# Last norm of the sample rows over 128 lanes of 256 columns, and their accumulating loads moved ahead of two prompt tiles

## What is computed

```
x = layer_norm(ALPHA * x + hier_moe(x, p), p['ln3_g'], p['ln3_b'])

def layer_norm(x, g, b):
    mu = xf.mean(-1, keepdims=True)
    var = jnp.mean(jnp.square(xf - mu), -1, keepdims=True)
    return (xf - mu) * lax.rsqrt(var + LN_EPS) * g + b
```

## Time and profile before

| | |
|---|---|
| median of 3 runs | 645.8 us (643.83 to 647.42) |
| the profiled execution | 641.11 us, span 639.4 us |
| mean granted clock of TensorE | 0.993 |
| busy, share of the span | PE 96%, DVE 57%, ACT 26%, POOL 32% |
| the chain that ended last, by engine | PE 76%, DVE 8%, DMA 7%, POOL 3% |
| DMA | 150.08 MB, mean 235 GB/s |

### The profile page before, as it was taken

How to read it: one execution, slowest core, us unless ns; L and a number is a source line. 1 busy time by engine, 2 the same in 40 slices (tenths; PEclk the granted TensorE clock), 3 DMA queues, 4 the chain that set the end, 5 groups by cost and what they waited for, 6 DMA issues and landing times.

```text
span 639.4 us, 9069 instructions
## 1 busy us (share of the span) xinstructions
PE 612.1 (96%) x3369; PEld 395.5 (62%) x3369; DVE 366.1 (57%) x847; ACT 163.7 (26%) x367; POOL 202.1 (32%) x248
## 2 busy tenths in 40 slices
PE   8999999999999999999999999999999999999992
PEld 5688788887788854446888774444574443333230
DVE  2476797327465863657553965356885342443465
ACT  1094401102553120002002640221433111211144
POOL 7040100101678735412001985011325731110231
PEclk9999999999999999999999999999999999999997
DMA  8995488706436354004705985453998999999898
GB/s 275 361 375 201 167 204 234 258 2 213 120 115 216 114 198 149 16 0 172 289 1 174 332 292 192 163 221 145 375 417 324 406 411 392 342 411 417 331 185 174
DMA packets 49181, 150.08 MB, mean 235 GB/s; under 512 B 5501, under 2 KB 8257, under 8 KB 44903
## 3 DMA queue, kind: packets, MB, share of 16 engines
q1 hardware_dynamic: 35159, 112.48, 47.2%
q0 software_dynamic: 11232, 31.76, 17.3%
q10 hardware_dynamic: 2744, 5.23, 2.2%
HBM read 131.83 MB, written 21.90 MB: 240 GB/s over the span
## 4 chain that ended last, share of the span: by engine, by line
PE 76%; DVE 8%; DMA 7%; POOL 3%; issue 2%; SPq 2%; ACT 1%; DVEq 0%; POOLq 0%; ACTq 0%
PE ps L618 16%; PE ps L797 14%; PE ps L1158 9%; PE ps L616 8%; PE ps L1178 6%; PE ps L517 5%; DMA xn<-in_x_sample 3%; PE ps L816 2%; PE ps L1196 2%; PE ps L899 2%; PE ps L591 2%; PE ps L883 2%; DMA P<-x_d,smp 1%; SPq L1284 1%; PE ps L1139 1%
## 5 line engine op out<-in xcount | busy, mean ns | idle before, releaser
L797 PE MATMUL ps<-wring,P 128*128 128x512 f32 x224 | 99.2, 596 | 0.0
L797 PEld LDWEIGHTS ps<-wring,P 128*128 128x128 f32 x224 | 41.6, 190 | 49.1 <-issue 49.0
L1938 DVE SCALAR_TENSOR_TENSOR P<-ps,P 128x256 f32<-128x256 f32 (+1 forms) x83 | 33.8, 424 | 56.6 <-PE ps L618 36.5
L1158 PE MATMUL ps<-wring,P 128*32 128x512 f32 (+1 forms) x320 | 63.5, 593 | 0.9 <-DVE P L2613 0.9
L517 PE MATMUL ps<-xT,wring 128*128 128x312 f32 (+1 forms) x256 | 57.4, 383 | 0.0
L517 PEld LDWEIGHTS ps<-xT,wring 128*128 128x128 f32 x256 | 46.4, 190 | 9.3
L2613 DVE COPY P<-ps 128x512 f32<-128x512 f32 x10 | 6.9, 692 | 64.7 <-PE ps L1139 64.7
L1158 PEld LDWEIGHTS ps<-wring,P 128*32 128x32 f32 (+1 forms) x320 | 20.4, 122 | 30.9 <-issue 30.9
L2935 POOL TENSOR_TENSOR P<-P,xT 128x2048 f32<-128x2048 f32 x8 | 36.1, 4522 | 8.8 <-DMA xT<-sq_d 5.4
L2787 POOL TENSOR_SCALAR rstd<-agg 128x1 f32<-128x1 f32 (+1 forms) x10 | 11.9, 1195 | 82.8 <-DVE agg L1867 82.8
L2246 DVE SCALAR_TENSOR_TENSOR xn<-xn,ps 128x512 f32<-128x512 f32 x16 | 11.0, 684 | 39.6 <-PE ps L797 29.0
(11 more groups left out here) (484 smaller groups left out, 1152.6 us busy)
## 6 DMA issues: line engine op xcount, KB each, us to landing
wring<-in_w_in SPq DMA_DIRECT2D x5, 2048.0 KB, 9.6
wring<-in_w_gate SPq DMA_DIRECT2D x10, 1024.0 KB, 8.3
wring<-in_w_up SPq DMA_DIRECT2D x10, 1024.0 KB, 11.2
P<-in_w_down SPq DMA_DIRECT2D x10, 1024.0 KB, 12.6
P<-in_cache_mem_k SPq DMA_DIRECT2D x8, 1024.0 KB, 6.8
P<-in_cache_mem_v SPq DMA_DIRECT2D x8, 1024.0 KB, 5.4
y_d<-P POOLq DMA_DIRECT2D x1, 4160.0 KB, 31.7
wring<-in_ca_wv SPq DMA_DIRECT2D x2, 2048.0 KB, 19.7
```

Source lines behind the costliest of these rows:

```text
L797: last = mm(bk[:, :], src[:, k, START[t]:START[t] + TR], w[:, k, :], start=(k == 0), stop=(k == KC - 1))
L1158: last = mm(GU[p % 2][lo:lo + m, :].rearrange("p (g f) -> p g f", g=2), xgT[:, p % 3, k, lo:lo + m], gu[s][:, :, k, :], start=(k == 0), st ...
L1938: V.scalar_tensor_tensor(dst, src, scale, part, ALU.mult, ALU.add).then_inc(part_added, 1)
```

## The change

- The samples' last norm is done on 128 partitions: row r's quarter g of 256 columns lies on partition 32g + r (the tile samples_s). SP moves the four quarters there from xn (four DMAs inside the on-chip memory) once the samples' second choice has landed. POOL clears samples_s earlier, and loads the gain in the same layout by four DMAs.
- VectorE adds the samples' sums straight from PSUM in one instruction of 128x256; mean, square and centring are one instruction of 256 columns each. The sums over the four quarters of a row are made by TensorE with a 0/1 matrix (same_lane, made in place_rows), once for the mean (after the sums of tile 1) and once for the variance (before the sums of tile 4): sum_lanes. The copies L1801 and L2700 are gone.
- LAST_NORM becomes [0, 1, 3, 2, 4], and ScalarE's list is written out.
- POOL's order of accumulating DMAs becomes: first choices of 3 and 0; wait for the first choice of 3; its second choice; first choices of 1, 2 and 4; then the second choices of 2 and 4 as before.
- POOL stores tiles 0, 1 and 2, and after them the samples in four DMAs of 8 rows of 256 columns.
- SP waits for three more output DMAs.

The code for a recomputation that runs when an expert gets too many rows isn't entered with these inputs; its counters change too.

```diff
-LAST_NORM = [0, 3, 1, 2, 4]
+LAST_NORM = [0, 1, 3, 2, 4]
+LANES = 32
...
-        kept_sums = lambda t, q: (1 if t == 0 else 2) + kept_bank(t, q)
-        SAMPLES_SUM = 3
+        kept_sums = lambda t, q: {0: 1, 1: 4, 2: 7, 4: 10}[t] + q
+        SAMPLES_SUM, SAMPLES_MEAN, SAMPLES_VAR = 3, 6, 9
...
+            def sum_lanes(column, parts):
+                mm(ps[0][:, column:column + 1], same_lane, parts, start=True, stop=True).then_inc(sum_full, 1)
...
             for t in PROMPT:
                 if t == 4:
-                    pe.wait_ge(y_act, NPASS + 1)
-                    pe.wait_ge(y_dve, NPASS + 1)
+                    pe.wait_ge(x3_square, 4)
+                    sum_lanes(1, square3[:, SAMPLES:SAMPLES + 1])
...
                 if t == 0:
                     add_samples(1, ps[6]).then_inc(sum_full, 1)
+                if t == 1:
+                    pe.wait_ge(row_parts, SAMPLES_ADDED)
+                    sum_lanes(0, part3[:, SAMPLES, 0:1])
...
+            sp.wait_ge(x3_in[SAMPLES], loads_of(SAMPLES))
+            for g in range(4):
+                sp.dma_start(samples_s[lanes(g), :], xn[0:NS, SAMPLES, quarter_of(g)]).then_inc(x_in, 16)
...
+            square(0)
+            root(0)
+            scale(0)
+            square(1)
+            root(1)
+            square(SAMPLES)
+            scale(1)
+            root(SAMPLES)
+            square(2)
+            root(2)
+            scale(SAMPLES)
+            scale(2)
+            square(4)
+            root(4)
...
             def place_rows(i):
                 p = NSCAT + i
+                if i == 0:
+                    link(V.tensor_reduce(lane_rows, ident.rearrange("p (g q) -> p q g", q=LANES), AX, ALU.add))
+                    V.tensor_copy(same_lane.rearrange("p (g q) -> p g q", g=4), lane_rows.unsqueeze(1).broadcast_to([128, 4, LANES])).then_inc(places_ready, 1)
...
+                if t == SAMPLES:
+                    dve.wait_ge(sum_full, SAMPLES_MEAN)
+                    V.tensor_scalar(mean, ps[0][:, 0:1], -1.0 / D, None, ALU.mult).then_inc(x3_mean, 1)
+                    dve.wait_ge(x3_mean, i + 1)
+                    V.scalar_tensor_tensor(centred_s, samples_s, mean, gain_s, ALU.add, ALU.mult).then_inc(x3_centred, 1)
+                    continue
+                x, centred = xn[:, t, :], centred3[:, t, :]
+                if t == 1:
+                    dve.wait_ge(x_in, RELAID)
+                    dve.wait_ge(sum_full, SAMPLES_SUM)
+                    add_rows(samples_s, ps[6][:, 0:256], part3[:, SAMPLES, 0:1])
...
+                if t == 2:
+                    take_root(SAMPLES)
...
             norm_vectors("ln3_g", "ln3_b")
+            link(G.memset(samples_s, 0.0))
+            for g in range(4):
+                pool.dma_start(gain_s[LANES * g:LANES * g + LANES, :], a["ln3_g"][0, quarter_of(g)].partition_broadcast(LANES)).then_inc(gb_in, 16)
             pool.wait_ge(zero_out, 16)
...
-            for t in (SAMPLES, 0, 1, 2):
-                accumulate(0, t)
+            accumulate(0, SAMPLES)
+            accumulate(0, 0)
             pool.wait_ge(x3_in[SAMPLES], 16)
             accumulate(1, SAMPLES)
+            accumulate(0, 1)
+            accumulate(0, 2)
             accumulate(0, 4)
...
-            for i, t in enumerate(LAST_NORM[:NT - 1]):
-                n = rows_of(t)
-                rows = o_xs.rearrange("b one d -> (b one) d") if t == SAMPLES else o_xp[0, START[t]:START[t] + TR, :]
+            for i, t in ((0, 0), (1, 1), (3, 2)):
                 pool.wait_ge(x3_scaled, i + 1)
-                pool.dma_start(rows, centred3[0:n, t, :], accum_op=ALU.add).then_inc(rows_out, 16)
+                pool.dma_start(o_xp[0, START[t]:START[t] + TR, :], centred3[:, t, :], accum_op=ALU.add).then_inc(rows_out, 16)
+            for g in range(4):
+                pool.dma_start(o_xs.rearrange("b one d -> (b one) d")[:, quarter_of(g)], centred_s[lanes(g), :], accum_op=ALU.add).then_inc(rows_out, 16)
```

More of the change, by code:

```diff
@@ L268, in layer_kernel @@
         centred3 = view(0, NT * D, "p (t d) -> p t d", t=NT)
-        late_samples = P[0:NS, NT * D:(NT + 1) * D]
+        gain_s, same_lane, lane_rows, samples_s = smp[:, 32:288], smp[:, 288:416], smp[:, 416:416 + LANES], smp[:, 544:800]
+        centred_s = view(NT * D, 256)
+        lanes = lambda g: slice(LANES * g, LANES * g + NS)
+        quarter_of = lambda g: slice(256 * g, 256 * g + 256)
+        RELAID = 16 * NT + 64
         zeros = view(16094, 256)
-        places = smp[:, 1120:1120 + KEPT * NTOK].rearrange("p (i c) -> p i c", i=KEPT)
-        tokens16 = smp[:, 2162:2162 + KEPT]
+        places = smp[:, 1120:1120 + KEPT * (NP_ + LANES)].rearrange("p (i c) -> p i c", i=KEPT)
+        tokens16 = smp[:, 2208:2208 + KEPT]
         squares = view(10464, D)
@@ L1415, in _ @@
             sp.wait_ge(half_out, 16)
-            sp.wait_ge(rows_out, 16 * NQT)
+            sp.wait_ge(rows_out, 16 * (NQT + 3))
             sp.wait_ge(out_done, 16 * 2)
@@ L1795, in _ @@
             act.wait_ge(x3_square, 1)
-            for i, t in enumerate(LAST_NORM):
-                n = rows_of(t)
[L1798 to L1811, removed]
+            nth = LAST_NORM.index
@@ new lines, in square, with root @@
+            def square(t):
+                act.wait_ge(x3_mean, nth(t) + 1)
+                n = 128 if t == SAMPLES else rows_of(t)
+                x = samples_s if t == SAMPLES else xn[0:n, t, :]
+                A(squares[0:n, 0:x.shape[1]], x, ACT.Square, bias=mean3[0:n, t:t + 1], accum_out=square3[0:n, t:t + 1]).then_inc(x3_square, 1)
+            def root(t):
+                if t == SAMPLES:
+                    act.wait_ge(sum_full, SAMPLES_VAR)
+                    total = ps[0][:, 1:2]
+                else:
+                    act.wait_ge(x3_square, nth(t) + 2)
+                    total = square3[:, t:t + 1]
+                A(rstd[:, t:t + 1], total, ACT.Sqrt, scale=1.0 / D, bias=eps).then_inc(x3_root, 1)
@@ new lines, in scale @@
+            def scale(t):
+                act.wait_ge(x3_rstd, nth(t) + 1)
+                act.wait_ge(x3_centred, nth(t) + 1)
+                centred = centred_s if t == SAMPLES else centred3[:, t, :]
+                A(centred, centred, ACT.Copy, scale=rstd[:, t:t + 1]).then_inc(x3_scaled, 1)
+            square(0)
[7 more added lines that the diff above has]
+            square(2)
@@ L2643, in place_rows @@
                 for t in range(NT):
-                    n = rows_of(t)
+                    n = LANES if t == SAMPLES else TR
                     last = V.tensor_scalar(places[:, i, START[t]:START[t] + n], slots16[:, 0:n], number, -float(NE * START[t]), ALU.subtract, ALU.is_equal)
@@ L2681, in _ @@
                     lo, hi = q * 512, q * 512 + 512
[L2682 to L2694, removed]
-                dve.wait_ge(x3_mean, i + 1)
[L2696 to L2701, removed]
+                    dve.wait_ge(sum_full, kept_sums(t, q))
+                    add_rows(x[:, lo:hi], ps[kept_bank(t, q)][:, :], part3[:, t, q:q + 1])
+                    if q == 0 and t != 0:
+                        take_root({1: 0, 2: 1, 4: 2}[t])
+                dve.wait_ge(row_parts, {0: 2, 1: 5, 2: 7, 4: 9}[t])
+                V.tensor_scalar(mean, part3[:, t, 0:1], part3[:, t, 1:2], -1.0 / D, ALU.add, ALU.mult).then_inc(x3_mean, 1)
+                dve.wait_ge(x3_mean, i + 1)
+                V.scalar_tensor_tensor(centred, x, mean, gb[:, 0, :], ALU.add, ALU.mult).then_inc(x3_centred, 1)
+                if t == 2:
+                    take_root(SAMPLES)
                 if i == NT - 1:
-                    take_root(i)
+                    take_root(t)
                     dve.wait_ge(x3_centred, i + 1)
```

28 lines of the change are left out of this document (15 added, 13 removed).

## The result

The changed kernel takes 649.8 us (median of 22 runs) against 647.3 for the kernel before (22 runs, made beside them). The ratio is 1.0057, with a 95% interval of 1.0038 to 1.0076: slower by 3.7 us (2.5 to 4.9). The ratio leaves out one slow run of the changed kernel; the medians, 2.5 us apart, say what stands at the lower end of the interval. The forecast was +2.5 us, 0.4%.

The account below looks back on a forecast made before the run. Tile 4's start on VectorE was taken to bound the end, set by POOL's queue of accumulating loads. Queue +1.75 and tail +0.75 gave +2.5 us on 645.8, so 648.3 us, range 644.4 to 651.0.

Parts of the forecast that it names:

- What bounds the end: Start of VectorE's tile 4: VectorE just in time, the queue 0.5 us ahead, TensorE 1.8; VectorE's net 2.7 us saving cancelled.
- The signs: Last norm: tile 1's buffered choice begins near 617.5, VectorE waits for xn before tile 2, samples' stores land last.
- POOL's queue: Accumulating loads of the last norm: tile 1's first choice lands 2.7 us late, tile 4 begins later by 1.75 us.
- The relaid samples: On-chip transfer of the samples before VectorE's addition: there at about 620, needed at 621.5; nothing, or 3 us at the far end.
- TensorE's stops: New waits for the samples' addition and square: tile 4's sums still ready ahead of use, costing nothing by 1 us.
- The third rival: TensorE's stops lower its clock to 1.2 GHz for tile 4's sums: +2.5 us on top, 650.8; chance 0.04.
- The tail: Stores at the kernel's end: the samples' four stores come last and land at T + 7.9 instead of T + 7.2, +0.75 us.
- The gain loads: POOL's clearing and four loads before the gather at 504.20: some 3 us, taken as covered, cost nothing.

Follow-up runs that it names:

- e4: The changed kernel with the clearing of samples_s and the four gain loads moved behind POOL's last scatter: +2.6 us on the kernel before (ratio 1.0040).
- e9: The changed kernel with SP's final wait for the stored rows put ahead of its waits for tile 4's halves: +5.4 us on the kernel before (1.0083).
- e10: The changed kernel with two of the samples' four on-chip DMAs issued by ACT instead of SP: +3.8 us on the kernel before (1.0059).
- e3: The changed kernel without the four stores of the samples' rows and SP's wait for them: +1.5 us on the kernel before (1.0024).
- e6: The kernel before with the samples' rows stored last, in four DMAs of 256 columns: +2.6 us on the kernel before (1.0041).
- e7: The kernel before with the samples' rows stored last, in one DMA of 8 whole rows: +2.8 us on the kernel before (1.0044).
- e2: The kernel before with only the clearing of samples_s and the four gain loads added in POOL's list, unread: 0 us (1.0001).
- e1: The kernel before with only POOL's new order of accumulating loads: 0 us (0.9999).
- e5: The changed kernel with POOL's old order of accumulating loads: +8.6 us on the kernel before (1.0133).
- e8: The changed kernel with the samples scaled ahead of tile 2's square and stored ahead of tile 2: +2.3 us on the kernel before (1.0035).
- e11: The changed kernel with the early samples' stores of e8 and the two-engine relay of e10: +3.7 us on the kernel before (1.0057).
- e12: The changed kernel with early samples' stores, relay issued by SP and ACT, and gain loads behind the last scatter: +1.6 us on the kernel before (1.0025).

## Why the prediction was right, and where its sizes were off

**What bounds the end.** The reading that the queue was 0.05 and 0.5 us ahead of VectorE, and TensorE 1.8, was borne out in the main: 2.7 us less work on VectorE bought nothing, and VectorE met all three kinds of wait that it named, the accumulating loads, the relaid samples and TensorE's sums. The signs came true in the changed kernel's profile: tile 1's buffered choice began 12.6 us after zero (12.9 by the forecast), VectorE waited for xn before tile 2, and the samples' stores landed last. From zero, VectorE ends tile 4's work at 29.95, 29.85, 29.8 and 30.0 in the changed kernel, e4, e9 and e10 (31.4 in e3), and at 29.0, 29.9, 30.0 and 30.5 in before, e6, e7 and e2. The means are 30.2 and 29.9.

**POOL's queue, +1.75: the right mechanism in the profile, too large.** Tile 1's choice came 2.45 us late (I said 2.7), the second choices went out at 16.1 and 18.0 from zero (15.9 and 18.7), VectorE stood 0.7 us before tile 2 (1.4), and tile 4 began 0.8 us later. The order alone (e1) gave 0 in the runs, so no run shows that it costs anything at the end. The excess has two parts. Tile 2's second choice landed 5.7 us after its issue where I took 6.5. And I let tile 4 wait for its own second choice; that was issued 0.6 us sooner than I had it, and VectorE went from tile 2 to tile 4 without a stand.

**The relaid samples, "nothing": too small.** VectorE stood 0.6 us for them, 1.0 to 1.7 in six others of the seven with this order of loads, since the four small DMAs took 8.2 us from SP's first issue (617.48) to VectorE's addition; I had said some 5. The samples' second choice itself landed in 3.5 us instead of my 5.1, which made up for part.

**TensorE's stops, nothing "by 1 us": right in this profile, but without the margin.** They were 0.98 and 0.72 us, and tile 4's sums were complete 0.04 us before their use, not 1. In all eight variants of the changed kernel VectorE did stand for the second half of tile 4's sums, 0.6 to 0.7 us in e3, e4, e5, e9 and e10 and 0.2 in e8, e11 and e12. Where it stood 0.6 to 0.7 us, TensorE's first stop, for the samples' addition behind the relay, had taken 1.3 to 4.7 us. So this path reached the end too, and not POOL's queue alone. The third rival didn't come in the changed kernel, where every stretch of 4 us from 612 to 636 was granted 1.00. It came in e3 and e5, where tile 2's sums took 5.4 and 6.7 us instead of 3.7. That is two of the nine profiles of the new layout, which makes my chance of 0.04 look too low.

**The tail, +0.75: the step that was mis-sized most.** It measured 3.6 us in the changed kernel's profile and 2.3 in the mean of the six kernels with four stores last (8.0 against 5.7); in the runs 2.6 (e6), 2.8 (e7) and 2.1 (e3 against the changed kernel). I priced only when the last small store would land, T + 7.9, where T is the end of tile 2's scaling. That was well read: in e4, e6 and e10 it landed at T + 7.7 or 7.8. The two errors in it cancelled, since the stores were issued 0.5 us apart instead of 0.80 and the last took 5.3 or 5.4 us instead of 4.4. The sum had no term for the engines' common end, which took 1.6 to 1.8 us more in all six. In the changed kernel's own profile there is a second part: the last small store took 6.6 us and landed at T + 9.0, and tile 4's halves, which I took as they were, needed 6.1 and 5.6 us. The Trainium skill ("DMA: Bandwidth & Descriptors", on the anatomy of one DMA) would have put a store of 8 KB at its fixed 2.0 us, by its fit an estimate that lands before the halves and is free; the trace doesn't agree, here the four took 4.8 to 6.6. Its rule to coalesce small transfers (the Trainium skill, same page, section "Rules for kernel authors") showed no gain in this place: one store (e7) cost about what four did.

**The gain loads, "at nothing": wrong by its own numbers.** I wrote that the gather at 504.20 is wanted at 520.28 and lands after at most 15 us. That is 519.2, a cover of 1 us, and the step then laid 3 us of new issues on it. The profiles show this pass 1.0 to 1.7 us longer in all eight kernels that have the loads there, and 1.1 in the mean with the pass before it. That it costs as much at the end isn't shown by the runs: e4 says 1.1 us, e2 nothing, both within their intervals.

**The sum.** Stores 2.1 to 2.8, gain loads 0 to 1.1, order and new layout about 0.3: 2.4 to 4.2, against 3.7 measured. The forecast was right in its sign and in its range. That 2.5 came so near is in part luck: the queue's term was 1 us too large, while the common end (1.7) and the gain loads (about 1 by the profiles) were missing. The measured 0.57% lies a little beyond the 0.5% that I called no change, to which I had given 0.63 against 0.32 for slower; the interval, 0.38 to 0.76%, covers both.

**Open:** why the common end of the engines takes 3.1 to 3.3 us in the kernels with four stores last and 1.4 to 2.0 in the others; the order of SyncE's waits isn't the cause. Why tile 4's halves took 5.4 to 6.1 us in the changed kernel and e7, and 3.8 to 4.9 beside the same kind of stores in e4, e5, e6, e9 and e10. Why e9, whose profile is no worse than e4's, ran at +5.4 us. And what makes TensorE's clock fall in e3 and not in e4.

## What to carry to other kernels

An engine that never waits may still be just in time: hold the landing of each of its inputs against its start before counting on its shorter work. The last stores of a kernel can cost more than their own landing: a small accumulating store moved behind the others cost 2.1 to 2.8 us here, whether in one piece or in four. With four, most of it stood in the engines' common end, which a view of landings alone doesn't show. A second queue helps only if its engine is free at that moment: look where the issue stands in its list. When work is added ahead of a DMA, subtract its landing time from the cover before calling it hidden, even where the engine that issues it seems idle.

## What was not expected of the hardware

- DMAs inside the on-chip memory are not short: 8 rows of 1 KB took 8.2 us from the first issue to their use, next to the accumulating loads, and SP spent 4.09 us on issuing four of them, where its two 512 KB loads took 0.82.
- A small DMA issued by POOL (8 or 32 KB to the output) took 4.1 to 6.6 us at the end of the kernel, about as long as the last one of 512 KB (5.1 to 5.4 in before, changed, e3, e6, e7 and e10).
- With four small accumulating stores last, the engines' common end took 3.1 to 3.3 us in six profiles, and 1.4 to 2.0 in the eight others.
- TensorE's granted clock fell after a stand of 1.8 us in e3 (0.63 over the next 4 us) and not after one of 2.0 in e4.
